# Router on transposed x, expert choice by pairwise ranks, and a gather signalled in pieces

## What is computed

```python
mix = rms_norm(mix, out_norm_w[l].reshape(N_MIX_GROUPS, HEAD_DIM)).reshape(b, s, D_MIX)
x = x + g1 * (mix @ w_out[l])
h2 = rms_norm(x, norm2_w[l]) * (1 + sc2) + sh2
x = x + g2 * hier_moe(h2, w_group[l], b_group[l], w_expert[l], b_expert[l], w1[l], w3[l], w2[l])
# in hier_moe:
g_prob = jax.nn.softmax((xt @ w_group + b_group).astype(jnp.float32), axis=-1)
g_top_p, g_top = lax.top_k(g_prob, 1)
e_in = jnp.take_along_axis(e_logits, g_top[:, :, None], axis=1)[:, 0]
e_top_p, e_top = lax.top_k(jax.nn.softmax(e_in, axis=-1), TOP_K)
...
return (jax.nn.silu(xb @ w1[e]) * (xb @ w3[e])) @ w2[e]
```

## Time and profile before

| | |
|---|---|
| median of 3 runs | 1762.76 us (1761.27 to 1765.35) |
| the profiled execution | 1751.8 us, its span 1750.0 us |
| PE busy, share of the span | 1381.0 us, 79% |
| PE weight loads | 861.6 us, 49% |
| DVE | 628.7 us, 36% |
| ACT | 164.3 us, 9% |
| bytes moved | 590.07 MB, mean 337 GB/s |
| chain that ended last | DMA 48%, PE 44%, DVE 5%, ACT 2% |

### The profile page before, as it was taken

The page is one execution under the profiler, slowest core; times in us unless marked ns, Lnnn a source line. Parts: engine busy times, 40 slices in busy tenths (PEclk is TensorE's granted clock), DMA queues, the critical chain, the costliest instruction groups (busy, mean ns, idle before and its releaser), DMA issues.

```text
span 1750.0 us, 24372 instructions
## 1 busy us (share of the span) xinstructions
PE 1381.0 (79%) x10631; PEld 861.6 (49%) x10631; DVE 628.7 (36%) x984; ACT 164.3 (9%) x413; POOL 5.0 (0%) x10
## 2 busy tenths in 40 slices
PE   6798998766676666766666567668998999889997
PEld 4787853322122212221222122216876999879997
DVE  2367642601010101010101010107446877768775
ACT  2003321100000000000000000002521000120001
POOL 1000000000000000000000000000000000000000
PEclk8998998888688868887888788889999999999999
DMA  9989957999999999999999999997944555414541
GB/s 401 365 335 402 407 230 298 396 431 431 431 431 431 431 431 431 431 431 431 431 431 431 431 431 431 431 430 282 404 164 151 206 207 188 172 70 164 210 176 63
DMA packets 46554, 590.07 MB, mean 337 GB/s; under 512 B 5360, under 2 KB 7824, under 8 KB 9376
## 3 DMA queue, kind: packets, MB, share of 16 engines
q1 hardware_dynamic: 42896, 583.89, 80.3%
q10 hardware_dynamic: 3600, 5.34, 0.9%
HBM read 586.58 MB, written 2.62 MB: 337 GB/s over the span
## 4 chain that ended last, share of the span: by engine, by line
DMA 48%; PE 44%; DVE 5%; ACT 2%; issue 1%; SPq 0%; DVEq 0%; ACTq 0%
DMA ring<-in_w 45%; PE ps L1985 5%; PE ps L1980 5%; PE ps L1981 5%; PE ps L1516 3%; PE ps L1689 3%; PE ps L1784 3%; PE ps L1804 3%; PE ps L1458 3%; PE ps L1996 2%; PE ps L1999 2%; PE ps L1998 2%; DMA ring<-in_w_in 2%; DMA ring<-in_w_ada 1%; DVE ring_parts L810 1%
## 5 line engine op out<-in xcount | busy, mean ns | idle before, releaser
L1784 PE MATMUL ps<-ring,mixT 128*32 128x512 f32 x2016 | 297.6, 726 | 166.6 <-DMA ring<-in_w 164.3
L1804 PE MATMUL ps<-ring,arena 128*32 128x512 f32 x1024 | 173.6, 815 | 106.3 <-DMA ring<-in_w 95.2
L1784 PEld LDWEIGHTS ps<-ring,mixT 128*32 128x32 f32 x2016 | 61.1, 121 | 377.1 <-DMA ring<-in_w 252.7
L810 DVE TENSOR_TENSOR ring_parts<-ring,ring_parts 128x1024 fp32r<-128x1024 f32 (+3 forms) x119 | 189.6, 1625 | 1.1
L1178 DVE TENSOR_TENSOR arena<-arena,ps 128x512 f32<-128x512 f32 x16 | 11.0, 687 | 495.8 <-PE ps L1784 495.8
L1980 PE MATMUL ps<-mixT_parts,ring_parts 128*128 128x256 f32 x704 | 171.0, 282 | 6.7 <-issue 6.7
L1981 PE MATMUL ps<-mixT_parts,ring_parts 128*128 128x256 f32 x704 | 170.8, 282 | 0.0
L1804 PEld LDWEIGHTS ps<-ring,arena 128*32 128x32 f32 x1024 | 33.0, 130 | 228.5 <-DMA ring<-in_w 146.5
L807 DVE CAST ring_parts<-ring 128x1024 fp32r<-128x1024 f32 (+3 forms) x119 | 100.3, 890 | 113.6 <-DMA ring<-in_f 72.2
L1980 PEld LDWEIGHTS ps<-mixT_parts,ring_parts 128*128 128x128 f32 x704 | 134.4, 191 | 7.9 <-issue 7.1
L1981 PEld LDWEIGHTS ps<-mixT_parts,ring_parts 128*128 128x128 f32 x704 | 134.0, 190 | 0.8
(11 more groups left out here) (359 smaller groups left out, 1374.0 us busy)
## 6 DMA issues: line engine op xcount, KB each, us to landing
ring<-in_w SPq DMA_DIRECT2D x190, 2048.0 KB, 25.7
ring<-in_ada_w SPq DMA_DIRECT2D x24, 2048.0 KB, 12.1
ring<-in_f SPq DMA_DIRECT2D x22, 2048.0 KB, 7.7
ring<-in_w_ada SPq DMA_DIRECT2D x12, 2048.0 KB, 16.5
ring<-in_f SPq DMA_DIRECT2D x22, 1024.0 KB, 5.5
ring<-in_w_in SPq DMA_DIRECT2D x5, 2048.0 KB, 22.9
ring<-in_w_out SPq DMA_DIRECT2D x2, 2048.0 KB, 11.4
ring<-in_mix_in SPq DMA_DIRECT2D x2, 2048.0 KB, 22.0
```

Of the source, the lines that this page charges most:

```text
L810: return tt(out.bitcast(F32R), v, hi, ALU.subtract)
L1784: last = mm(ps[rows[u], j, :], XeT[:, 2 * m + k, rows[u]], w[:, u, k * FE:(k + 1) * FE], start=(m == 0 and k == 0), stop=(m == 3 and k == 1))
L1804: last = mm(ps[rows[u], m, :], heT[:, k, rows[u]], w[:, u, m * 512:(m + 1) * 512], start=(k == 0), stop=(k == FE // P - 1))
```

## The change

- The gate g1 is spread (`gate_row`) and copied to `gB` before the first attention round, not ahead of the projection.
- PE transposes x itself, tile by tile, as soon as it is there; ACT and DVE copy it to `hT` without scale or shift. The scale is multiplied into the router's weights (`wrA`, in the space of `Ye`); the shift's part is a product of `Bcol` and `wr`, made between the two last parts of the projection and added to the bias `brB`; 1/rms multiplies the router's results.
- The gather reads the normed, unmodulated `xn`; scale and shift are put on the gathered columns when `gathered` evicts them, here and in the loop (eight operations of 128 columns where one of 1024 stood). The second set of transposes and ACT's copies of it are gone.
- The two best experts come from ranks: each of the eight is compared with all eight, with ties broken by index (`before8`), in place of two rounds of maxima. The mask is made first; what only the gate weights need comes after the first `select`, partly after the first gather.
- The second `gate_row` stands behind the router, and its wait (`g_ev` 2) and the zero matmuls ahead of the ranks. Dummy matmuls of 256 columns (`busy`) stand before that wait and behind the ranks.
- `Ssel` and `SG` are signalled apart; the gather signals after each half, the eviction after each quarter, and PE waits for each quarter at its use. SP's side load waits for `xT_ev` 2 and `g_mm` 2, the context weights for `lg_mm`.

```diff
...
         Ye = take(D)
+        wrA = Ye[:, 256:256 + KD * 72].rearrange("p (k n) -> p k n", k=KD)
+        before8 = prod[:, 384:448].rearrange("p (i j) -> p i j", i=8)
+        above, equal = (prod[:, n:n + 128].rearrange("p (t i j) -> p t i j", t=NT, i=8) for n in (128, 256))
         assert at[0] <= 5120
...
                 elif n == SIDE[1]:
-                    sp.wait_ge(g_ev, 1)
+                    sp.wait_ge(xT_ev, 2)
                     sp.wait_ge(g_mm, 2)
                     sp.dma_start(side[1], src).then_inc(side_in[1], 16)
-                    sp.wait_ge(h2_tr, 1)
+                    sp.wait_ge(lg_mm, 1)
                     sp.dma_start(rk, span(A["mix_in"], MIX_CUTS[2], MIX_CUTS[3])[0]).then_inc(context_in, 16)
...
             queries(0)
+            act.wait_ge(g_mm, 1)
+            nc.scalar.activation(gB[:, :], ps[:, 4:6, :].rearrange("p b n -> p (b n)"), ACT.Copy).then_inc(g_ev, 1)
             act.wait_ge(win_act, 4)
...
             nc.scalar.activation(modrow[:, 256:512], modrow[:, 2816:3072], ACT.Copy)
-            act.wait_ge(g_mm, 1)
-            nc.scalar.activation(gB[:, :], ps[:, 0:2, :].rearrange("p b n -> p (b n)"), ACT.Copy).then_inc(g_ev, 1)
...
-            norm(1, after(1))
-            norm_out(1, 4)
+            nc.scalar.activation(warm, epsc, ACT.Sqrt)
+            for t in range(NT):
+                act.wait_ge(x_new, t + 1)
+                link(nc.scalar.activation(xn[:, t, :], x[:, t, :], ACT.Square, accum_out=ss[:, t:t + 1]))
+                nc.scalar.activation(sd2[:, t:t + 1], ss[:, t:t + 1], ACT.Sqrt, scale=1.0 / D, bias=epsc
+                                     ).then_inc(nrm_sq, 1)
+                if t == 0:
+                    for b in range(2):
+                        act.wait_ge(xT_tr, b + 1)
+                        nc.scalar.activation(hT[:, 4 * b:4 * b + 4, 0:P],
+                                             ps[:, 2 + b, :].rearrange("p (k n) -> p k n", n=P), ACT.Copy
+                                             ).then_inc(xT_ev, 1)
+            act.wait_ge(x_new, NT)
+            act.wait_ge(g_mm, 2)
+            nc.scalar.activation(gB[:, :], ps[:, 6:8, :].rearrange("p b n -> p (b n)"), ACT.Copy).then_inc(g_ev, 1)
             act.wait_ge(lg_gx, 1)
             nc.scalar.activation(r8[1], r8[0], ACT.Exp).then_inc(lg_ex, 1)
-            act.wait_ge(h2_tr, 1)
-            for t in range(NT):
-                last = nc.scalar.activation(xn[:, t, :], ps[:, 4 + 2 * t:6 + 2 * t, :].rearrange("p b n -> p (b n)"),
-                                            ACT.Copy)
-            last.then_inc(h2_ev, 1)
             act.wait_ge(lg_gx, 2)
             nc.scalar.activation(r1[4], r1[3], ACT.Exp).then_inc(lg_ex, 1)
-            act.wait_ge(x_new, NT)
-            act.wait_ge(g_mm, 2)
-            nc.scalar.activation(gB[:, :], ps[:, 2:4, :].rearrange("p b n -> p (b n)"), ACT.Copy).then_inc(g_ev, 1)
...
             last.then_inc(at_mix, 1)
-            nc.vector.memset(Ye, 0.0).then_inc(at_mix, 1)
+            nc.vector.memset(Ye[:, 0:256], 0.0).then_inc(at_mix, 1)
+            dve.wait_ge(col_ev, 3)
+            modulation(modcol[:, 0, 16:32], V("norm2"))
+            dve.wait_ge(misc_in, 64)
+            dve.wait_ge(mod_ready, 2)
+            tt(wrA, wr[:, :, :], Acol.unsqueeze(2).to_broadcast([P, KD, 72]), ALU.mult).then_inc(at_mix, 1)
+            link(tt(before8, C("iota")[:, 0:8].unsqueeze(2).to_broadcast([P, 8, 8]),
+                    C("iota")[:, 0:8].unsqueeze(1).to_broadcast([P, 8, 8]), ALU.is_gt))
...
                     else:
+                        link(tt(brB[:, :], ps[:, 0, 144:216], brB[:, :], ALU.add))
                         done(dve, RO + 1)
...
-            dve.wait_ge(col_ev, 3)
-            modulation(modcol[:, 0, 16:32], V("norm2"))
+            for b, ready in enumerate(((xT_tr, 3), (nrm_tr, 2))):
+                dve.wait_ge(*ready)
+                nc.vector.tensor_copy(hT[:, 4 * b:4 * b + 4, P:T], ps[:, 4 + b, :].rearrange("p (k n) -> p k n", n=P)
+                                      ).then_inc(nrm_hT, 1)
...
-            norm_out(1, 4)
-            dve.wait_ge(misc_in, 64)
-            dve.wait_ge(lg_mm, 1)
...
-            link(tt(lg, ps[:, 0, 0:144].rearrange("p (t e) -> p t e", t=NT),
-                    brB[:, :].unsqueeze(1).to_broadcast([P, NT, 72]), ALU.add))
...
-            def first_max(onehot, v, m):
...
-                link(nc.vector.tensor_reduce(mx, tmp8, AX.X, ALU.max))
-                link(tt(onehot, tmp8, b2(mx), ALU.is_equal))
+            dve.wait_ge(lg_mm, 1)
+            for t in range(NT):
+                last = stt(lg[:, t, :], ps[:, 0, t * 72:(t + 1) * 72], rstd[:, t:t + 1], brB[:, :], ALU.mult, ALU.add)
+            link(last)
...
-            tt(gx, lgg, b2(gmax), ALU.subtract).then_inc(lg_gx, 1)
-            first_max(onehot_g, lgg, w2c)
+            link(tt(tmp8, lgg, b2(gmax), ALU.is_equal))
+            link(tt(tmp8, tmp8, rev, ALU.mult))
+            link(nc.vector.tensor_reduce(mx, tmp8, AX.X, ALU.max))
+            link(tt(onehot_g, tmp8, b2(mx), ALU.is_equal))
...
-            first_max(o1, ein, w1c)
+            own = ein.unsqueeze(3).to_broadcast([P, NT, 8, 8])
+            other = ein.unsqueeze(2).to_broadcast([P, NT, 8, 8])
+            tt(above, other, own, ALU.is_gt)
+            link(tt(equal, other, own, ALU.is_equal))
+            link(tt(equal, equal, before8.unsqueeze(1).to_broadcast([P, NT, 8, 8]), ALU.mult))
+            link(tt(above, above, equal, ALU.add))
+            link(nc.vector.tensor_reduce(tmp8, above, AX.X, ALU.add))
+            link(ts(o2, tmp8, 2.0, None, ALU.is_lt))
+            mt = msk.rearrange("p t (g e) -> p t g e", g=8)
+            tt(mt, onehot_g.unsqueeze(3).to_broadcast([P, NT, 8, 8]), o2.unsqueeze(2).to_broadcast([P, NT, 8, 8]),
+               ALU.mult).then_inc(lg_mask, 1)
+            tt(gx, lgg, b2(gmax), ALU.subtract).then_inc(lg_gx, 1)
+            link(ts(o1, tmp8, 0.0, None, ALU.is_equal))
+            nc.vector.tensor_reduce(w1c, ein, AX.X, ALU.max)
...
-            first_max(o2, e2, w2c)
+            link(nc.vector.tensor_reduce(w2c, e2, AX.X, ALU.max))
...
-            link(tt(tmp8, o1, o2, ALU.add))
-            mt = msk.rearrange("p t (g e) -> p t g e", g=8)
-            tt(mt, onehot_g.unsqueeze(3).to_broadcast([P, NT, 8, 8]), tmp8.unsqueeze(2).to_broadcast([P, NT, 8, 8]),
-               ALU.mult).then_inc(lg_mask, 1)
...
-            link(tt(gat[:, :, 0:E].rearrange("p t (g e) -> p t g e", g=8),
-                    onehot_g.unsqueeze(3).to_broadcast([P, NT, 8, 8]), o1.unsqueeze(2).to_broadcast([P, NT, 8, 8]),
-                    ALU.mult))
...
-            rk = ps[:, 1, 0:128].rearrange("p (t e) -> p t e", t=NT)
-            link(tt(rnk[:, :, 0:E], rk, msk, ALU.mult))
+            link(tt(rnk[:, :, 0:E], ps[:, 1, 0:128].rearrange("p (t e) -> p t e", t=NT), msk, ALU.mult))
+            four = lambda ap: ap.rearrange("p t (e s) -> p t e s", e=QD)
+            per_slot = lambda ap, cols: ap[:, :, cols].unsqueeze(3).to_broadcast([P, NT, QD, SLOTS])
...
-                four = lambda ap: ap.rearrange("p t (e s) -> p t e s", e=QD)
...
-                bc = lambda ap: ap[:, :, cols].unsqueeze(3).to_broadcast([P, NT, QD, SLOTS])
...
-                    last = tt(four(Ssel)[:, t], bc(rnk)[:, t], iota, ALU.is_equal)
-                link(last)
+                    last = tt(four(Ssel)[:, t], per_slot(rnk, cols)[:, t], iota, ALU.is_equal)
+                last.then_inc(S.sel, 1)
+            def weigh(S, cols, selected):
+                dve.wait_ge(S.sel, selected)
...
-                    last = tt(four(SG)[:, t], four(Ssel)[:, t], bc(gat)[:, t], ALU.mult)
+                    last = tt(four(SG)[:, t], four(Ssel)[:, t], per_slot(gat, cols)[:, t], ALU.mult)
...
-            def gathered(S, v):
-                dve.wait_ge(S.tok, v)
-                nc.vector.tensor_copy(XeT, ps[:, 2:4, :].rearrange("p b (k s) -> p (b k) s", s=P)).then_inc(S.tokT, 1)
+            def gathered(S, i, ahead):
+                for b in range(2):
+                    dve.wait_ge(S.tok, S.th(i, 2, b + 1, ahead))
+                    for k in range(4):
+                        last = ts(XeT[:, 4 * b + k, :], ps[:, 2 + b, k * P:(k + 1) * P], Acol[:, 4 * b + k:4 * b + k + 1],
+                                  Bcol[:, 4 * b + k:4 * b + k + 1], ALU.mult, ALU.add)
+                        if k % 2:
+                            last.then_inc(S.tokT, 1)
...
-                    gathered(S, S.th(i))
+                    gathered(S, i, 0)
...
                 select(S, cols)
+                weigh(S, cols, S.th(i, 2, 1, 1))
                 S.units(dve, i, 12)
...
                 if more:
-                    gathered(S, S.th(i) + 1)
+                    gathered(S, i, 1)
+            select(first, slice(0, QD))
             link(nc.vector.tensor_copy(cnt, ps[:, 1, 128:192]))
-            select(first, slice(0, QD))
-            gathered(first, 1)
```

(87 more changed lines are left out.)

37 lines of the change are left out of this document (10 added, 27 removed).

## The result

| | before | after |
|---|---|---|
| median | 1762.39 us (1754.93 to 1765.57, 7 runs) | 1746.16 us (1742.27 to 1748.56, 7 runs) |
| ratio after to before | | 0.9907, 95% interval 0.9892 to 0.9922 |
| profiled execution, its span | 1751.8, 1750.0 | 1745.32, 1743.5 |
| DVE busy | 628.7 | 653.4 |

The change takes 16.2 us off the median; 11.6 were forecast. The sum for the stretch that it was made for came out within 0.3 us. What failed is its last line, the base it was taken from.

A forecast was written before the change was run, and what follows sets the result against it. The expert weight stream was taken as the bound, its start set by PE's first expert matmul. Terms 0 + 6.4 + 1.0 + 1.25 + 0.8 + 0.9 + 1.3 = 11.6 us off 1762.76 gave 1751.2, range 1747 to 1759.

The forecast's parts named there:

- Item 1: Around the projection: the gate row leaves (1.78 us), eight broadcast matmuls for the router's bias enter (1.78); net 0.
- Item 2: Projection's end to router's end: transposing x instead of the modulated norm, with the router at full clock, gains 6.4 us.
- Item 3: Router to mask: pairwise ranks and mask first take 4.4 us instead of 5.4, gaining 1.0.
- Item 4: PE between router and ranks: its 4.1 to 4.3 us are covered by the mask; rank passes at full clock gain 1.25.
- Item 5: Ranks to first expert matmul: selection gains 0.8 us net, gather at full clock 0.9, XeT's copy off the path 1.3.
- Item 6: Early part: gate_row fits PE's idle time ahead of the first queries; taken as 0, between -1.7 and +1.1 us.
- Item 7: SP's queue: unit 7 and the context weights go out at other times but land before they are needed; cost 0.
- Item 8: Expert loop: eight scalings replace one XeT copy, hidden behind output matmuls; cost 0, or up to 15 x 1.2 us.
- The stream's start sets the end: Expert weight stream: each microsecond by which PE's first expert matmul comes earlier is a microsecond off the end.
- Rival C: Expert loop: quads wait for DVE's scaled copy, 18 us less the gain, giving 1769; chance 0.05.
- Rival A: Projection to gather: PE's clock falls all the same, gain shrinks to 2 to 8 us, middle 1757.8; chance 0.20.
- the last line of the sum: Whole kernel: takes 11.6 us off both profiled span and median, giving span 1738.4 and median 1751.2.

The follow-up runs named there:

- b_early: Kernel before with only the first gate_row and its copy moved ahead of the attention rounds; median 1760.81 us, ratio 0.9999.
- a_norank: Changed kernel with the two rounds of maxima in place of the pairwise ranks; median 1746.2 us, stretch to the first expert matmul 17.02.
- b_again: Kernel before, unchanged, run and profiled once more; median 1763.72 us, ratio 1.0006.
- a_whole: Changed kernel with signalling in pieces undone, so copies and the first expert matmul wait for the whole; median 1746.33 us.
- a_again: Changed kernel as it is, run again; median 1743.16 us, ratio to before 0.9908.
- a_late: Changed kernel with 22 dummy matmuls of 256 columns between the first gather and the first expert matmul; median 1755.07 us.
- b_shift: Kernel before with 13 unneeded matmuls of 64 columns in PE's wait near 34 us; median 1757.68 us, ratio 0.9982.
- b_pad8: Kernel before with 8 unread matmuls of 64 columns (32 instructions) in PE's wait near 34 us; median 1758.52 us, ratio 0.9977.
- b_pad1: Kernel before with a single unread matmul of 64 columns (4 instructions) in PE's wait near 34 us; median 1758.21 us, ratio 0.9984.
- a_nofill: Changed kernel without its five dummy matmuls; median 1745.78 us.
- b_fill: Kernel before with 13 dummy matmuls of 256 columns in PE's three waits between projection and ranks; median 1755.9 us, ratio 0.9973.
- a_short14: Changed kernel with 14 matmuls (56 instructions) of the modulation's first block left out near 24 us; median 1747.93 us, ratio to before 0.9917.
- a_short: Changed kernel with 8 matmuls (32 instructions) of the modulation's first block left out near 24 us; median 1744.01 us.

## Why the prediction was right, and where it was wrong

| step | forecast | measured |
|---|---|---|
| 2: projection's end to router's end | 12.1 less 6.4 | 5.8, less 6.3 |
| 3: router to mask | 4.4 | 4.36 (256.87 to 261.23) |
| 4: ranks | 1.25 | 1.37 (261.23 to 262.60) |
| 5: selection | 0.8 less | 1.75 to 0.96, 0.8 less |
| 5: gather and copy | 2.2 less | 5.78 to 3.75, 2.0 less |
| sum | 11.6 | 11.3 |

*Item 1 (net 0)* held: the projection stretch is 30.59 against 30.29, and 29.01 in b_early, where the gate row alone is gone: 1.3 from the one, 1.6 back to the other.

*Item 2* held by its own working; the last transposes waited 0.27 and the four loads of wr and evictions hid as costed. The router took 3.7.

*Item 3* held, and a_norank measured it alone at 0.8.

*Item 4* held: PE's work between router and ranks ended at 260.9 and the ranks waited 0.36 for the mask, so it was covered, by little, as forecast. Without the dummies nothing moved.

*Item 5* held: 3.75 from the gather's start to the first expert matmul, and 3.0 lost when the pieces are waited for as a whole, where the gather's part of the item was 0.9 by the clock and 1.3 by the copy. The pieces hide more than the old copy cost, since the eight scalings (2 x 1.37) are dearer than the one copy they replace (1.3).

*Item 6.* I took 0 between -1.7 and +1.1. In after the clock falls later in the first scores (0.82 over 158 to 160.5, where before has 0.50 over 156 to 159.9), which take 2.4 us (158.06 to DVE's start at 160.44) instead of 3.8, but nothing of it arrives: the way from the first scores to the projection is 62.4. That way took 60.9 in before, b_again and a_whole, 62.1 to 62.7 in after, a_again, a_late, b_early and b_shift, and 63.6 to 64.1 in the rest, b_pad8 and b_pad1 among them. The clock rows part the three levels. Ahead of the projection it falls once more, at 213 to 218 us, in every kernel but the three with 60.9:

```profile
213.00:220.00 7.00, 7.00 (x43) 5.19 (x43) 4.08 (x8) 1.28 (x1) 0.00 (x0) 1.00 1.03 427
```

```profile
213.00:220.00 7.00, 7.00 (x35) 6.76 (x35) 1.43 (x3) 0.00 (x0) 0.00 (x0) 0.52 0.99 418
```

The upper row is before, the lower b_pad8; after has 0.83 there. In all, PE runs 8.5 to 9.0 us at half clock on that way where it takes 60.9, 9.2 to 13.1 where it takes 62.1 to 62.7, and 12.4 to 16.2 in the rest. a_whole has the early gate row and 60.9, b_pad8 has it not and 64.1, so it is not the row's price; b_early, which makes this edit alone, has a median equal to before's. So 0 stands; why the clock falls there in some and not in others is open.

*Item 7 (0)* held: unit 7 and the context weights went out at 258.75 and 259.12, the queue restarted at 269.29, 1.98 behind the first expert matmul, as before.

*Item 8 (0)* held: in 700 us of the loop DVE is busy 78.8 instead of 60.6, PE 469.2 and the stream 431 GB/s as before. Rival C is out.

*The stream's start sets the end* held: 879 to 882 us from restart to mix_in in every kernel, and a_late moved the end by what it moved the start.

*Rival A, the clock falls,* did not come: 1.00 throughout, also in a_nofill. The rule that I weighed (the Trainium skill, "TensorE: Matmul & The Clock Gate", Part 4: transposes don't count as PE work for the clock) is not contradicted by it, since only 2.4 us of transposes stand between projection and router; but as a forecast of this stretch it pointed the wrong way, and the lengths of the waits pointed the right way. b_fill keeps the clock at 1.00 with 32 transposes and dummy matmuls in the waits, which fits the rule as well as the waits, so no run here parts the two.

**The step that failed** is the last line of the sum: "I take the sum off both: span 1738.4, median 1762.76 - 11.6". The profiled execution lay 11 us under the median, and I took that for spread that the change would leave alone. Part of it was not. In before's layout a wait for instructions stands behind the experts: 1.8 us in the execution whose profile I read, and 7.0 (a start 1.8 late, then the stop of 5.24) in b_again, which lies near the median. The cheap case stood in the profile's own chain as 1.77 us of "issue", and I passed over it. After has 1.6 there. Measured: 51.60 to 44.74 in that stretch, so 6.9 of the 16.7 between the spans of b_again and after. 5.4 of the 6.9 are the waits (7.0 less 1.6), 1.2 an earlier first `xn` (29.2 instead of 30.4; a_again has 30.5, so it does not come with the change every time), 0.3 the transposes themselves. With the stretch's 11.3, the start's 0.9 and the stream's 0.7, less 1.6, 0.3 and 1.2 elsewhere, that is the whole 16.7, near the 16.2 of the medians. Moving the packets alone, with nothing of the change, gave ratios of 0.9977 (0.9961 to 0.9993, b_pad8), 0.9982 (0.9965 to 0.9999, b_shift) and 0.9984 (0.9965 to 1.0003, b_pad1), about 3 to 4 us, each in spite of a router stretch that was 1.6 to 3 longer.

How large the step's share of the miss is in the medians stays uncertain. By its interval the change's gain is 13.7 to 19.0 us beside the runs that it was measured with. Beside the 31 runs with 1759.19, a_nofill, which is the change without dummies, has a ratio of 0.9934 (0.9911 to 0.9956), 7.7 to 15.7 us: there the forecast 11.6 would have stood. What is shown is that the wait exists, that it swings by 5 us between executions of before, and that its large case is in no profile of the change or its variants but a_short14, which was made for it.

Against the profile that I had, the span came out 5.1 over the forecast 1738.4: the start was 2.0 later and the end 2.7 longer (b_again differs from it by 2.9 and 1.5 in the same rows, with no edit), the way to the projection 1.6 longer. So one profiled execution is a base only to some 3 us for any of these.

Not settled: why a_short has no stop though its first packet is back at before's place (by the count of instructions its edge should lie within the run), why the packet near +24 comes 5.4 later in one execution of before than in the other, and why the clock falls earlier behind the projection in b_pad1, b_pad8 and b_shift. That the packets' place decides is shown, by one profile each, in before (one matmul moves the stop, eight remove it) and in after (14 fewer bring it in); the exact count is not.

## What to carry to other kernels

Where the weights' stream stands still while a chain of small operations ends, sum that chain step by step from rows of both clock levels: here it held to 0.3 us over five steps. Before taking a sum off a median, ask what the profiled execution and the median differ by, and look for "issue" inside a run of equal instructions while the DMA queues are full: it may be an instruction packet, whose cost swings between executions, and which an edit far away adds or removes. See whether a packet lies 2 to 3 us ahead of where the run goes on; the two gaps of 3.33 us that every profile here has at one line late in the span (L1980 in before) are marked "issue" too, and no packet lies so close ahead of them. When comparing two kernels to within a few microseconds, compare stretches between common points, not totals, since 32 added instructions that compute nothing moved the total by 1 to 7 us here.

## What the runs showed of the hardware

- PE's instructions come in packets of 16 KB, 46 in the span, by a DMA queue of their own on the same 16 engines. Under a stream of 430 GB/s they are 5.5 to 6.0 us apart when wanted one after the other, and PE goes on 2.2 to 2.5 us after one starts (3.7 once, in b_pad1). Whether the stream makes them late was not tested.
- In this program 32 more instructions moved the packet ahead of mix_in by 4.6 us, the time of one weight unit (b_pad8); 4 more moved it by 4.8 in b_pad1. That the edge lay just where PE passes from one unit to the next there is inferred, not shown.
- The clock stayed at 1.00 over waits of 1.40 and 1.00 us (a_nofill), and fell in before after waits of 0.83 and 2.02 with one of 0.33 between them. With 17.1 us at half clock behind the projection instead of 13.65, the old order took 29.2 to 30.6 us instead of 27.5 (b_pad1, b_pad8, b_shift); with none at half it took 25.3 (b_fill).
